# Token mixing of a hybrid decoder layer: the keys undivided until after the scores, and the turns of a tile moved behind them

## Chip, cores and metric

The kernel runs on one NeuronCore of a Trainium2 chip. The metric is the device time of one execution in microseconds (us); lower is better. The kernel before takes 2807.51 us, the median of three executions (2806.45 to 2814.20).

## The reference

One decoder layer over 2048 tokens of width 1024, in float32. One input projection feeds an RWKV-7 group (8 heads of 64) and a sliding-window attention group (8 query heads of 64, window 128). An output projection, a squared-ReLU MLP of width 4096 and a gated per-layer embedding follow. What the change touches is the RWKV group:

```python
kk = (k * k_k).reshape(B, S, H, N)
kk = kk / jnp.maximum(jnp.linalg.norm(kk, axis=-1, keepdims=True), 1e-12)
k = k * (1.0 + (a - 1.0) * k_a)
# per token and head, state is 64 x 64
sa = einsum('bhvk,bhk->bhv', state, -kk_t)
state = state * w_t + sa * (kk_t * a_t) + v_t * k_t
y = einsum('bhvk,bhk->bhv', state, r_t)
# after a group norm of y:
y = y + sum(r * k * r_k, axis=-1) * v
```

## The kernel before

**The work.** The kernel computes the scan in chunks of 64 tokens, two chunks in a tile of 128 tokens, 16 tiles in all. In a tile the decayed factors are called alpha (minus the key kk, times a decay), beta (kk times a, times the inverse decay), kappa (the modified key k, times the inverse decay) and rho (r, times a decay). Their pairwise products are the scores; masked, they give a triangular matrix per head and chunk that is inverted in blocks of 32 in five levels (products `mz0` to `mz4` on PE, L709; `z`, `up` and a transpose on DVE, L1499 to L1506), then joined to 64 (`q`, `b`, `xt64`). Then `uw`, `sa0`, `grow0`, `sa1`, `grow1` carry the state through the two chunks, and `y`, a group norm, `out` and `rw` end the tile. Attention of the same 128 tokens runs in between: `att0`, `att1` (L613), the soft maximum on DVE and ACT, and `pv` (L621).

**Large products.** The projection, the output product, the MLP and the gate (called the fill) are products of 128x128 by 128x512 in a split of each operand into a high and a low part, three products each (L590 to L594, L824 to L828, L866 to L870). A weight chunk of 512 KB is loaded three chunks ahead by SP (L376), its high part is written by ACT (L986) and its low part by DVE (L1300). The fill works in blocks of 512 tokens: `proj` 0 to 3, then `fin` 0 to 3.

**The order.** Every engine runs the same interleaving, written out by hand. `whole_program` runs `proj(0)` alone, then `proj(1)` to `proj(3)` beside the mixing of tiles 0 to 3, then `fin(b - 1)` beside the four tiles of block b, and `fin(3)` alone. A tile is a generator of 28 steps (`MIX_STEPS`), the fill is a generator of slots, most of them 12 large products on PE. The tuples `BESIDE_PROJ` (4 tiles) and `BESIDE_FIN` (4 tiles, used for three blocks) say for each step how many slots of the fill precede it. Steps of equal number have nothing of the fill between them. Each engine is in order, so a step whose input is late holds up all that stands behind it on that engine.

**The steps of a tile before the change.** Step 0: ACT tanh and sigmoid on the loaded rows (L1085, L1086), DVE the raw key (L1426), ACT its square (L1088). Step 1: PE `lora` (L639, L640) and `gate` (L643). Step 2: PE `norm` (L650), sums of squares per head, behind a wait for ACT's `sw`; ACT root (L1097); DVE running sum of the decay (`cum`, L1430) and `ascale` (L1434). Step 3: DVE reciprocal (L1440), ACT spreads it over 512 columns into `alpha_t` (L1100) and computes the exponentials; DVE `cumx`, `kmod`, `v_t`. Step 4: PE `spread`, four transposes of the widened reciprocal (L657); DVE multiplies the raw key by it (`kk`, L1451), then `kka`. Step 5: DVE alpha, beta, rk, kappa (L1457 to L1465). Step 6: PE `bonus` (L664) and twelve transposes of beta, alpha, kappa (L627); DVE `ends`, `rho`. Step 7: DVE `yb` and the copies `alpha_t`, `kappa_t` out of the banks. Step 8: PE scores (L684), DVE masks (L1485). Step 9: PE `av` (L696) and `att0`; DVE `init` (L1492), the first level, and the first attention logits. Steps 10 to 14: the levels. 15 `q`, 16 `b`, 17 `pv`, 18 `uw` (L744, L749), 19 `sa0` (L757), 20 `grow0` (L765), 21 `sa1`, 22 `grow1` and the inner part of y, 23 `y`, 26 `out` and `rw`.

```python
def side_by_side(fill, tiles, places):
    given = 0
    for i, place in enumerate(places):
        while given < place:
            next(fill)
            given += 1
        next(tiles[i // MIX_STEPS])
```

PE uses four banks for a tile, M0 to M3; before the change the scores could overwrite them only once `yb`, `beta_t`, `alpha_t` and `kappa_t` were out.

## Time and profile before

| | |
|---|---|
| executions | 2807.51 us median, 2806.45 to 2814.20, three |
| the profiled execution | 2812.94 us, span 2810.9 us |
| PE busy | 98% of the span, 25170 products |
| DVE, ACT busy | 62%, 40% |
| granted clock of PE, mean | 0.990 |

Busy time of PE is the union of its products' modelled durations. Products overlap, so the cost of one is read from the distance between starts. In the page a row reads: line, engine, operation, output and inputs, shapes, count, busy time, mean, idle time before it and what ended that.

### The profile page before, as it was taken

How to read it: one execution, taken by the hardware profiler on the slowest of the kernel's cores; microseconds unless marked ns; L12 is line 12 of the kernel's file. 1: busy time of each engine (PE TensorE's matmuls, PEld its weight loads, DVE VectorE, ACT ScalarE, POOL GpSimd, SP SyncE). 2: the span in 40 equal slices, each digit the busy share in tenths (PEclk: the TensorE clock that was granted, in tenths of full speed). 3: DMA queues.
4: the chain of work that ended last, by engine and by line, in shares of the span. 5: the costliest groups of instructions: out<-in, count | busy, mean ns of one | idle time of the engine just before them, and what ended most of it. 6: DMA issues, size and time to landing. Idle time of an engine off the chain costs nothing.

```text
span 2810.9 us, 57536 instructions
## 1 busy us (share of the span) xinstructions
PE 2748.7 (98%) x25170; PEld 2225.7 (79%) x25170; DVE 1742.8 (62%) x2941; ACT 1110.4 (40%) x1871; POOL 0.2 (0%) x4
## 2 busy tenths in 40 slices
PE   8999999999999999999999999999999999999998
PEld 6877787777878787878787878777888788888876
DVE  5477776757666566685766666857575655444335
ACT  4344443344433342553333424633433344332225
POOL 0000000000000000000000000000000000000000
PEclk9999999999999999999999999999999999999999
DMA  6554544453233233442333233523232234333332
GB/s 197 149 168 113 167 118 132 120 169 109 81 101 101 86 98 96 150 145 87 104 96 98 83 103 128 159 76 110 87 105 84 88 115 157 98 97 97 95 101 75
DMA packets 376197, 319.13 MB, mean 114 GB/s; under 512 B 48747, under 2 KB 328460, under 8 KB 375948
## 3 DMA queue, kind: packets, MB, share of 16 engines
q1 hardware_dynamic: 372272, 312.63, 36.5%
q8 instruction: 198, 3.24, 0.5%
q10 hardware_dynamic: 3676, 2.84, 0.4%
q14 instruction: 51, 0.42, 0.0%
HBM read 277.65 MB, written 38.14 MB: 112 GB/s over the span
## 4 chain that ended last, share of the span: by engine, by line
PE 73%; DVE 3%; ACT 2%; DMA 1%; issue 1%; SPq 0%; ACTq 0%
PE ps L824 13%; PE ps L828 12%; PE ps L827 12%; PE ps L866 9%; PE ps L869 8%; PE ps L870 8%; PE ps L709 1%; DMA wraw_f<-in_w_gate 1%; PE ps L684 1%; PE ps L621 1%; PE ps L765 1%; PE ps L837 1%; PE ps L757 1%; PE ps L627 1%; PE ps L613 1%
## 5 line engine op out<-in xcount | busy, mean ns | idle before, releaser
L1300 DVE TENSOR_TENSOR w_lo<-wraw_f,w_hi 128x1024 fp32r<-128x1024 f32 x408 | 498.0, 1221 | 357.3 <-ACT w_hi L986 356.4
L986 ACT ACTIVATE w_hi<-wraw_f 128x1024 fp32r<-128x1024 f32 x408 | 430.2, 1054 | 624.2 <-PE ps L824 505.9
L824 PE MATMUL ps<-w_hi,h_hi 128*128 128x512 f32 x1280 | 518.4, 405 | 10.8 <-DVE act_lo L1642 10.0
L828 PE MATMUL ps<-w_hi,h_lo 128*128 128x512 f32 x1280 | 501.8, 392 | 0.0
L827 PE MATMUL ps<-w_lo,h_hi 128*128 128x512 f32 x1280 | 501.6, 392 | 0.0
L866 PE MATMUL ps<-act_hi,w_hi 128*128 128x512 f32 x1024 | 408.4, 399 | 1.5 <-DVE w_lo L1300 1.4
L869 PE MATMUL ps<-act_lo,w_hi 128*128 128x512 f32 x1024 | 399.2, 390 | 0.0
L870 PE MATMUL ps<-act_hi,w_lo 128*128 128x512 f32 x1024 | 398.9, 390 | 0.0
L824 PEld LDWEIGHTS ps<-w_hi,h_hi 128*128 128x128 f32 x1280 | 241.7, 189 | 67.8 <-issue 16.9
L828 PEld LDWEIGHTS ps<-w_hi,h_lo 128*128 128x128 f32 x1280 | 241.7, 189 | 53.0
L827 PEld LDWEIGHTS ps<-w_lo,h_hi 128*128 128x128 f32 x1280 | 242.0, 189 | 46.0 <-issue 0.3
L1180 ACT ACTIVATE h_hi<-tmp 128x512 fp32r<-128x512 f32 x128 | 80.8, 631 | 462.3 <-DVE tmp L1633 462.3
L866 PEld LDWEIGHTS ps<-act_hi,w_hi 128*128 128x128 f32 x1024 | 192.1, 188 | 46.3 <-issue 4.1
L870 PEld LDWEIGHTS ps<-act_hi,w_lo 128*128 128x128 f32 x1024 | 192.2, 188 | 41.1
L869 PEld LDWEIGHTS ps<-act_lo,w_hi 128*128 128x128 f32 x1024 | 192.4, 188 | 37.3
L1636 DVE TENSOR_TENSOR h_lo<-tmp,h_hi 128x512 fp32r<-128x512 f32 x128 | 88.7, 693 | 156.8 <-ACT tmp L1181 156.8
L1633 DVE SCALAR_TENSOR_TENSOR tmp<-ps,stage_f 128x512 f32<-128x512 f32 x128 | 88.2, 689 | 137.7 <-PE ps L870 135.6
L590 PE MATMUL ps<-act_hi,w_hi 128*128 128x512 f32 x320 | 132.4, 414 | 0.0
L824 PE MATMUL ps<-w_hi,act_hi 128*128 128x512 f32 x320 | 127.3, 398 | 2.7 <-DVE w_lo L1300 2.4
L590 PE MATMUL ps<-h_hi,w_hi 128*128 128x512 f32 x320 | 128.4, 401 | 0.5 <-DVE h_lo L1311 0.5
L593 PE MATMUL ps<-act_lo,w_hi 128*128 128x512 f32 x320 | 127.8, 399 | 0.0
L594 PE MATMUL ps<-act_hi,w_lo 128*128 128x512 f32 x320 | 127.4, 398 | 0.0
(227 smaller groups left out, 3939.2 us busy)
## 6 DMA issues: line engine op xcount, KB each, us to landing
wraw_f<-in_w_ff_up SPq DMA_DIRECT2D x256, 256.0 KB, 3.3
wraw_f<-in_w_ff_down SPq DMA_DIRECT2D x128, 512.0 KB, 3.8
wraw_f<-in_w_in SPq DMA_DIRECT2D x80, 512.0 KB, 4.4
zT<-tmp SPq DMA_DIRECT2D x80, 256.0 KB, 2.1
wraw_f<-in_w_out SPq DMA_DIRECT2D x32, 512.0 KB, 4.1
wraw_f<-in_w_gate SPq DMA_DIRECT2D x32, 512.0 KB, 4.5
zs<-zT SPq DMA_DIRECT2D x16, 896.0 KB, 6.5
h_lo<-mixT SPq DMA_DIRECT2D x4, 2048.0 KB, 8.0
```

Source lines behind the costliest of these rows:

```text
L590: mm = T.matmul(dst, wh, hi[:, k, :], start=(k == 0), stop=False)
L593: T.matmul(dst, wh, lo[:, k, :], start=False, stop=False)
L594: mm = T.matmul(dst, wl, hi[:, k, :], start=False, stop=(k == DK - 1))
L824: mm = T.matmul(ps[:, j, :], ah, wh, start=(first and k == 0), stop=False)
L827: T.matmul(ps[:, j, :], ah, wl, start=False, stop=False)
L828: mm = T.matmul(ps[:, j, :], al, wh, start=False, stop=(final and k == 1))
L866: mm = T.matmul(ps[:, bank, :], wh, act_hi[:, k, :], start=(k == 0), stop=False)
L869: T.matmul(ps[:, bank, :], wh, act_lo[:, k, :], start=False, stop=False)
L870: mm = T.matmul(ps[:, bank, :], wl, act_hi[:, k, :], start=False, stop=(k == DK - 1))
L986: S.activation(w_hi[:, n % 2, :], raw[:, n % 4, :], ACT.Copy).then_inc(w_hi_done, 1)
L1300: V.tensor_tensor(w_lo[:, n % 2, :], raw[:, n % 4, :], w_hi[:, n % 2, :].bitcast(F32), ALU.subtract).then_inc(w_lo_done, 1)
L1636: V.tensor_tensor(h_lo[:, i, :], tmp[:, i % 2, :], h_hi[:, i, :].bitcast(F32), ALU.subtract).then_inc(fin_dve.mark(f"h_lo{g}_{i}"), 1)
```

## The change

1. The key is not divided by its norm before the scores. ACT's root (`nrm`) and the spreading (`kk_wide`), PE's `spread` and DVE's `kk` are gone. `norm` joins step 1 and goes to bank M2; its wait for `sw` is gone.
2. The inverse square of the norm is a factor per row: `init` becomes four products with it instead of four copies, a product `corner` over the right half of each head's first score block is new, and the copies `sa0` and `sa1` out of the banks become products with it.
3. The scores stand in step 5, directly on the factors, and the twelve transposes of beta, alpha, kappa behind them in step 6, in front of `av`. The copies `alpha_t`, `kappa_t` (DVE) and `beta_t` (ACT) are in step 6 too.
4. `bonus` and `att0` stand behind `mz0` in step 7, with `yb` in step 7 on DVE.
5. A tile has 25 steps. Both tuples of places are new; SP's load of the next tile's rows (`load_rw`) stands in step 8 in place of 9, still behind `yb`. All later steps are renumbered by minus 3.

The diff, without the renumbered rest, indentation reduced:

```diff
-MIX_PE = (["lora", "gate", "norm", "spread", "bonus", "beta", "alpha", "kappa"] + upto("score", 4) + ["av", "att0", "mz0", "mz1", "att1",
+MIX_PE = (["lora", "gate", "norm"] + upto("score", 4) + ["beta", "alpha", "kappa", "av", "mz0", "bonus", "att0", "mz1", "att1",
            "mz2", "mz3", "mz4", "q", "b", "pv", "uw",
            "sa0", "grow0", "sa1", "grow1", "y_in", "y", "out"])
-MIX_ACT = ["tanh", "sig_g", "kk_sq", "sw", "av", "nrm", "kk_wide", "p_inc", "p_inv", "p_exc", "gate", "beta_t", "avt",
+MIX_ACT = ["tanh", "sig_g", "kk_sq", "sw", "av", "p_inc", "p_inv", "p_exc", "gate", "beta_t", "avt",
            "exp0", "esink0", "exp1", "esink1", "att", "y_rms"]
...
-MIX_DVE = (["kk_raw", "cum", "ascale", "kk_max", "kk_inv", "cumx", "kmod", "v_t", "kk", "kka", "alpha", "beta", "rk", "kappa", "ends", "rho", "yb", "alpha_t", "kappa_t"]
-           + upto("mask", 4) + ["init", "up0", "m0"] + logits_of(0) + level_of(1) + ["v_turn"] + level_of(2) + probs_of(0) + level_of(3) + logits_of(1)
-           + level_of(4) + [f"z{LEVELS}", "inv_t", "inv", "xt64", "q"] + probs_of(1)
+MIX_DVE = (["kk_raw", "cum", "ascale", "kk_max", "kk_inv", "cumx", "kmod", "kka", "v_t", "alpha", "beta", "rk", "kappa", "ends", "rho"]
+           + upto("mask", 4) + ["init", "up0", "m0", "alpha_t", "kappa_t", "corner"] + level_of(1) + logits_of(0) + ["yb", "v_turn"] + level_of(2)
+           + level_of(3) + probs_of(0) + level_of(4) + logits_of(1) + [f"z{LEVELS}", "inv_t", "inv", "xt64", "q"] + probs_of(1)
            + ["b", "wT", "sa0", "grow0", "state0", "sa1", "grow1", "state1", "y_sum", "y_mean", "y", "y_sq", "y_var", "y_inv", "y_norm", "rw", "rw_yb", "rw_gate"])
-MIX_STEPS = 28
+MIX_STEPS = 25
...
-BESIDE_PROJ = (5, 6, 6, 6, 6, 6, 8, 9, 12, 15, 17, 19, 19, 21, 24, 26, 27, 29, 30, 31, 32, 33, 34, 34, 34, 35, 37, 37, 37, 39, 39,
-               39, 40, 40, 42, 42, 43, 44, 45, 46, 47, 49, 52, 55, 56, 58, 59, 61, 62, 63, 64, 64, 65, 65, 68, 69, 70, 73, 73, 75,
-               76, 76, 79, 79, 80, 81, 83, 84, 85, 86, 87, 88, 89, 90, 90, 90, 90, 91, 92, 92, 93, 93, 95, 97, 97, 98, 98, 98, 98,
-               98, 100, 101, 102, 103, 104, 106, 107, 109, 111, 112, 113, 114, 114, 114, 114, 115, 116, 116, 117, 118, 119, 119)
-BESIDE_FIN = (0, 1, 2, 4, 4, 4, 6, 6, 8, 9, 10, 12, 13, 15, 19, 23, 24, 26, 29, 31, 33, 35, 36, 37, 37, 38, 39, 39, 40, 40, 41, 46,
-               46, 46, 48, 48, 49, 50, 52, 53, 54, 55, 58, 61, 62, 64, 65, 67, 68, 69, 70, 70, 72, 72, 73, 74, 74, 75, 76, 80, 80,
-               80, 82, 82, 84, 85, 87, 91, 95, 97, 100, 102, 103, 104, 105, 106, 107, 108, 109, 109, 110, 110, 112, 113, 113, 114,
-               114, 117, 120, 125, 127, 133, 134, 135, 136, 137, 138, 140, 141, 142, 143, 144, 145, 146, 148, 149, 150, 150, 151,
-               153, 158, 158)
+BESIDE_PROJ = (4, 6, 6, 7, 7, 10, 12, 15, 16, 18, 20, 22, 24, 26, 27, 28, 29, 30, 32, 33, 33, 34, 35, 36, 37, 37, 40, 40, 41, 42, 44,
+               45, 45, 46, 47, 49, 50, 51, 53, 54, 55, 56, 57, 58, 59, 59, 59, 59, 61, 62, 63, 64, 64, 65, 65, 68, 70, 71, 74, 75,
+               76, 77, 79, 80, 81, 82, 83, 84, 85, 86, 86, 87, 87, 89, 90, 91, 92, 92, 93, 93, 96, 99, 100, 101, 103, 104, 105, 107,
+               109, 110, 111, 112, 113, 114, 115, 115, 117, 118, 119, 119)
+BESIDE_FIN = (0, 2, 2, 3, 4, 6, 7, 8, 9, 11, 13, 18, 21, 22, 24, 26, 27, 28, 31, 33, 33, 33, 35, 37, 39, 40, 40, 40, 42, 42, 44, 46,
+               47, 48, 49, 50, 52, 57, 58, 60, 61, 65, 66, 67, 70, 70, 73, 73, 76, 78, 78, 78, 78, 79, 79, 82, 83, 84, 86, 89, 93,
+               96, 99, 102, 105, 106, 109, 110, 111, 112, 112, 113, 114, 116, 116, 117, 122, 122, 123, 127, 130, 133, 134, 135, 136,
+               137, 138, 139, 140, 142, 144, 146, 147, 148, 149, 149, 151, 156, 158, 158)
...
             load_qkv(t + 1)
-        if step == 9 and t < TILES - 1:
+        if step == 8 and t < TILES - 1:
             sp.wait_ge(*mix_pe.done(t, "gate"))
             sp.wait_ge(*mix_dve.done(t, "yb"))
             load_rw(t + 1)
-        if step == 19:
...
     mm.then_inc(mix_pe.mark("gate"), 1)
-    yield
-    after(mix_act, "sw")
     after(mix_act, "kk_sq")
     for f in range(PAIRS):
-        mm = T.matmul(ps[:, M3, 2 * f:2 * f + 2], four(T1)[:, f, :], ones[:, 0:P:HD], start=True, stop=True)
+        mm = T.matmul(ps[:, M2, 2 * f:2 * f + 2], four(T1)[:, f, :], ones[:, 0:P:HD], start=True, stop=True)
     mm.then_inc(mix_pe.mark("norm"), 1)
     yield
     yield
-    after(mix_act, "kk_wide")
-    for f in range(PAIRS):
-        mm = T.transpose(ps[:, M3, f * P:(f + 1) * P], alpha_t[:, f * P:(f + 1) * P], ident)
-    mm.then_inc(mix_pe.mark("spread"), 1)
     yield
     yield
     after(mix_act, "gate")
-    after(mix_dve, "rk")
-    T.matmul(ps[:, M0, :], ones[:, :], work[:, KK, :], start=True, stop=True).then_inc(mix_pe.mark("bonus"), 1)
-    tokens_major("beta", M1, four(AV))
-    tokens_major("alpha", M2, pp[:, 0, :, :])
-    after(mix_dve, "kappa")
-    tokens_major("kappa", M3, four(KM))
-    yield
-    yield
-    after(mix_dve, "yb")
     after(mix_dve, "rho")
-    after(mix_dve, "v_t")
-    after(mix_act, "beta_t")
-    after(mix_dve, "alpha_t")
-    after(mix_dve, "kappa_t")
     for g in range(2):
         for f in (2 * g, 2 * g + 1):
             for src, at in ((four(AV), 0), (four(KM), 2 * CH)):
...
     after(mix_dve, "mask1")
     after(mix_dve, "mask2")
     after(mix_dve, "mask3")
+    tokens_major("beta", M1, four(AV))
+    tokens_major("alpha", M2, pp[:, 0, :, :])
+    tokens_major("kappa", M3, four(KM))
...
     mm.then_inc(mix_pe.mark("av"), 1)
-    pe.wait_ge(qkv_in, 16 * (2 + P // SUB) * (t + 1))
-    scores(0)
     yield
     for l in range(LEVELS):
...
         mm.then_inc(mix_pe.mark(f"mz{l}"), 1)
+        if l == 0:
+            after(mix_dve, "kappa_t")
+            T.matmul(ps[:, M3, :], ones[:, :], work[:, KK, :], start=True, stop=True).then_inc(mix_pe.mark("bonus"), 1)
+            after(mix_act, "beta_t")
+            pe.wait_ge(qkv_in, 16 * (2 + P // SUB) * (t + 1))
+            scores(0)
         if l == 1:
             after(mix_dve, "logit0")
             scores(1)
...
-        if step == 2:
-            after(mix_pe, "norm")
-            S.activation(knorm[:, :], ps[:, M3, 0:HEADS], ACT.Sqrt).then_inc(mix_act.mark("nrm"), 1)
         if step == 3:
-            after(mix_dve, "kk_inv")
-            S.activation(alpha_t[:, :].rearrange("p (h d) -> p h d", h=HEADS), over(knorm[:, :], HD), ACT.Copy).then_inc(
-                mix_act.mark("kk_wide"), 1)
             after(mix_dve, "cum")
...
             if t:
                 act.wait_ge(att_stored, 16 * t)
             S.activation(pp[:, 0, :, :], four(SW), ACT.Exp, scale=-DECAY).then_inc(mix_act.mark("p_exc"), 1)
-        if step == 4:
             if t:
                 act.wait_ge(*mix_dve.done(t - 1, "rw_gate"))
             copy("gate", gate[:, :, :], ps[:, M1, :].rearrange("p (f t) -> p f t", f=PAIRS), "gate")
         if step == 6:
             copy("beta_t", beta_t[:, :], ps[:, M1, :], "beta")
-        if step == 9:
+        if step == 6:
             copy("avt", avt, ps[:, M0, :], "av")
-        if step in (10, 13):
-            exps(step // 13)
-        if step == 17:
+        if step in (8, 11):
+            exps(step // 11)
+        if step == 14:
...
     def chunk_of_sa(c):
         after(mix_pe, f"sa{c}")
-        V.tensor_copy(sa[tok64(c), :].rearrange("p (f a v) -> p a f v", a=2, v=HD),
-                      ps[tok64(c), M2:M2 + 2, 0:PAIRS * HD].rearrange("p a (f v) -> p a f v", f=PAIRS)).then_inc(mix_dve.mark(f"sa{c}"), 1)
+        key = knorm[tok64(c), :].rearrange("p (f a) -> p a f", a=2).unsqueeze(3).broadcast_to([CH, 2, PAIRS, HD])
+        V.tensor_tensor(sa[tok64(c), :].rearrange("p (f a v) -> p a f v", a=2, v=HD),
+                        ps[tok64(c), M2:M2 + 2, 0:PAIRS * HD].rearrange("p a (f v) -> p a f v", f=PAIRS), key,
+                        ALU.mult).then_inc(mix_dve.mark(f"sa{c}"), 1)
     def chunk_of_state(c):
         after(mix_pe, f"grow{c}")
...
-        if step == 3:
-            after(mix_act, "nrm")
-            V.tensor_scalar(knorm[:, :], knorm[:, :], 1e-12, None, ALU.max).then_inc(mix_dve.mark("kk_max"), 1)
+            after(mix_pe, "norm")
+            V.tensor_scalar(knorm[:, :], ps[:, M2, 0:HEADS], 1e-24, None, ALU.max).then_inc(mix_dve.mark("kk_max"), 1)
             own("kk_max")
             V.reciprocal(knorm[:, :], knorm[:, :]).then_inc(mix_dve.mark("kk_inv"), 1)
+        if step == 3:
...
+            own("kk_raw")
+            V.tensor_tensor(four(AV), four(KK), four(AV), ALU.mult).then_inc(mix_dve.mark("kka"), 1)
...
             V.transpose(v_t[:, :], kappa_t[:, :]).then_inc(mix_dve.mark("v_t"), 1)
         if step == 4:
-            after(mix_pe, "spread")
-            V.tensor_tensor(work[:, KK, :], work[:, KK, :], ps[:, M3, :], ALU.mult).then_inc(mix_dve.mark("kk"), 1)
-            own("kk")
-            V.tensor_tensor(four(AV), four(KK), four(AV), ALU.mult).then_inc(mix_dve.mark("kka"), 1)
-        if step == 5:
             after(mix_act, "p_exc")
-            own("kk")
             V.scalar_tensor_tensor(pp[:, 0, :, :], four(KK), -1.0, pp[:, 0, :, :], ALU.mult, ALU.mult).then_inc(mix_dve.mark("alpha"), 1)
             after(mix_dve, "kka")
             V.tensor_tensor(four(AV), four(AV), four(PINV), ALU.mult).then_inc(mix_dve.mark("beta"), 1)
...
             o.then_inc(mix_dve.mark("rk"), 1)
             own("rk")
             V.tensor_tensor(four(KM), four(KM), four(PINV), ALU.mult).then_inc(mix_dve.mark("kappa"), 1)
-        if step == 6:
             V.tensor_copy(ends[:, :, :], pp[:, 1, :, :].rearrange("p f (c t) -> p f c t", c=2)[:, :, :, CH - 1]).then_inc(
                 mix_dve.mark("ends"), 1)
             own("ends")
             V.tensor_tensor(pp[:, 1, :, :], r, pp[:, 1, :, :], ALU.mult).then_inc(mix_dve.mark("rho"), 1)
-        if step == 7:
-            after(mix_pe, "bonus")
-            if t:
-                dve.wait_ge(*mix_dve.done(t - 1, "rw_gate"))
-            V.tensor_tensor(yb[:, :, :], ps[:, M0, :].rearrange("p (f t) -> p f t", f=PAIRS), v, ALU.mult).then_inc(mix_dve.mark("yb"), 1)
-            after(mix_pe, "alpha")
-            V.tensor_copy(alpha_t[:, :], ps[:, M2, :]).then_inc(mix_dve.mark("alpha_t"), 1)
-            after(mix_pe, "kappa")
-            own("v_t")
-            V.tensor_copy(kappa_t[:, :], ps[:, M3, :]).then_inc(mix_dve.mark("kappa_t"), 1)
-        if step == 8:
+        if step == 5:
...
-        if step == 9:
+        if step == 6:
             own("mask3")
+            own("kk_inv")
             for i in range(4):
                 at = (i % 2) * SUB
-                o = V.tensor_copy(xx[sub32(i), 1, :, :].rearrange("p (a f) t -> p f a t", a=2),
-                                  bm[sub32(i), :, 0, at:at + SUB].rearrange("p (f a) t -> p f a t", a=2))
+                o = V.tensor_tensor(xx[sub32(i), 1, :, :].rearrange("p (a f) t -> p f a t", a=2),
+                                    bm[sub32(i), :, 0, at:at + SUB].rearrange("p (f a) t -> p f a t", a=2),
+                                    over(knorm[sub32(i), :], SUB).rearrange("p (f a) t -> p f a t", a=2), ALU.mult)
             o.then_inc(mix_dve.mark("init"), 1)
-        if 9 <= step < 9 + LEVELS:
-            l = step - 9
+        if 6 <= step < 6 + LEVELS:
+            l = step - 6
...
-        if step == 9:
+        if step == 6:
+            after(mix_pe, "alpha")
+            V.tensor_copy(alpha_t[:, :], ps[:, M2, :]).then_inc(mix_dve.mark("alpha_t"), 1)
+            after(mix_pe, "kappa")
+            own("v_t")
+            V.tensor_copy(kappa_t[:, :], ps[:, M3, :]).then_inc(mix_dve.mark("kappa_t"), 1)
+            own("init")
+            V.tensor_tensor(bm[:, :, 0, SUB:], bm[:, :, 0, SUB:], over(knorm[:, :], SUB), ALU.mult).then_inc(mix_dve.mark("corner"), 1)
+        if step == 7:
             logits(0)
-        if step == 10:
+            after(mix_pe, "bonus")
+            if t:
+                dve.wait_ge(*mix_dve.done(t - 1, "rw_gate"))
+            V.tensor_tensor(yb[:, :, :], ps[:, M3, :].rearrange("p (f t) -> p f t", f=PAIRS), v, ALU.mult).then_inc(mix_dve.mark("yb"), 1)
...
```

## Rows read from the trace of the kernel before

**Rows 1.** The page, busy time of each engine.

```profile
PE 2748.7 (98%) x25170; PEld 2225.7 (79%) x25170; DVE 1742.8 (62%) x2941; ACT 1110.4 (40%) x1871; POOL 0.2 (0%) x4
```

**Rows 2.** Waits of PE: who waited for whom, us in total, times, longest.

```profile
PE ps L639 <- ACT zs L1086: 7.1, 2, 4.0
PE ps L657 <- ACT alpha_t L1100: 4.3, 2, 2.6
...
PE ps L765 <- DVE work L1407: 1.6, 2, 0.8
PE ps L757 <- DVE work L1551: 1.6, 2, 0.8
PE ps L744 <- ACT pp L1080: 1.6, 2, 0.8
PE ps L560 <- DVE rw L1582: 1.5, 1, 1.5
```

**Rows 3.** Windows: busy time of PE, PEld, DVE, ACT, POOL; granted clock, DMA.

```profile
153.00:167.00 14.00, 11.87 (x50) 10.36 (x51) 10.53 (x26) 11.93 (x24) 0.00 (x0) 0.51 0.57 184
458.00:500.00 42.00, 39.22 (x301) 32.03 (x300) 30.06 (x63) 20.34 (x32) 0.00 (x0) 0.89 0.32 89
556.00:564.00 8.00, 6.43 (x73) 5.19 (x67) 3.45 (x5) 1.06 (x1) 0.00 (x0) 0.79 0.39 106
600.00:618.00 18.00, 14.92 (x68) 12.21 (x68) 10.06 (x15) 13.62 (x22) 0.00 (x0) 0.81 0.71 254
618.00:1120.00 502.00, 497.70 (x5322) 399.95 (x5322) 324.15 (x558) 184.30 (x323) 0.00 (x0) 1.00 0.32 95
```

**Rows 4.** Timeline of PE in the first tile: start, us, what, idle before.

```profile
149.05 0.39 PE L594 MATMUL ps<-act_hi,w_lo 128*128 128x512 f32 x1
153.43 0.58 PE L639 MATMUL ps<-zs,lora 64*128 64x128 f32 x1 [3.99 <-ACT zs L1086]
```

**Rows 5.** Timeline of SP at the same place.

```profile
138.78 0.39 SPq L403 DMA_DIRECT2D zs<-zT  x1
```

**Rows 6.** DMA issues from 130 to 160 us, KB, us to landing.

```profile
zs<-zT SPq DMA_DIRECT2D x1, 896.0 KB, 5.8
```

**Rows 7.** Timeline of ACT at the same place.

```profile
149.08 1.06 ACT L986 ACTIVATE w_hi<-wraw_f 128x1024 fp32r<-128x1024 f32 x1 [4.44 <-DMA wraw_f<-in_w_in]
```

**Rows 8.** Timeline of PE, large products right after the stall at 489 us.

```profile
493.43 0.63 PE L593 MATMUL ps<-act_lo,w_hi 128*128 128x512 f32 x1
493.86 0.63 PE L594 MATMUL ps<-act_hi,w_lo 128*128 128x512 f32 x1
```

**Rows 9.** Timeline of PE around one spread.

```profile
624.60 0.39 PE L827 MATMUL ps<-w_lo,h_hi 128*128 128x512 f32 x1
624.83 0.39 PE L828 MATMUL ps<-w_hi,h_lo 128*128 128x512 f32 x1
...
625.72 0.39 PE L827 MATMUL ps<-w_lo,h_hi 128*128 128x512 f32 x1
```

**Rows 10.** Timeline of PE around one mz product.

```profile
1222.22 0.39 PE L828 MATMUL ps<-w_hi,h_lo 128*128 128x512 f32 x1
1222.54 0.75 PE L709 MATMUL ps<-work,small 32*32 32x32 f32 x64
1223.23 0.50 PE L824 MATMUL ps<-w_hi,h_hi 128*128 128x512 f32 x1
1223.56 0.39 PE L827 MATMUL ps<-w_lo,h_hi 128*128 128x512 f32 x1
```

**Rows 11.** Timeline of PE, gate of the fourth tile.

```profile
487.16 1.16 PE L643 MATMUL ps<-zs,gup 128*128 128x128 f32 x8
```

**Rows 12.** Timeline of DVE there, from cum to kappa (11 groups between them lie close).

```profile
488.45 1.37 DVE L1430 TENSOR_TENSOR_SCAN work<-con,work 128x128 f32<-128x128 f32 x4
...
497.43 0.69 DVE L1465 TENSOR_TENSOR work<-work 128x512 f32<-128x512 f32 x1
498.04 1.22 DVE L1300 TENSOR_TENSOR w_lo<-wraw_f,w_hi 128x1024 fp32r<-128x1024 f32 x1
```

More of the change, by code:

```diff
@@ L448, in mix @@
                     for step in range(MIX_STEPS):
-                        if step == 14 and t < TILES - 1:
+                        if step == 11 and t < TILES - 1:
                             sp.wait_ge(*mix_pe.done(t, "att1"))
                             load_qkv(t + 1)
-                        if step == 9 and t < TILES - 1:
+                        if step == 8 and t < TILES - 1:
                             sp.wait_ge(*mix_pe.done(t, "gate"))
@@ L455, in mix @@
                             load_rw(t + 1)
-                        if step == 19:
+                        if step == 16:
                             sp.wait_ge(*mix_act.done(t, "att"))
                             sp.dma_start(mixT[PAIRS:, :, t * P:(t + 1) * P].rearrange("f p t -> p f t"), attT).then_inc(att_stored, 16)
-                        if step == 23 and t < TILES - 1:
+                        if step == 20 and t < TILES - 1:
                             sp.wait_ge(*mix_pe.done(t, "grow1"))
                             load_v(t + 1)
-                        if step == 27:
+                        if step == 24:
                             sp.wait_ge(*mix_dve.done(t, "rw_gate"))
@@ L1514, in mix @@
                                 mix_dve.mark("v_turn"), 1)
-                        if step == 11:
+                        if step == 9:
                             probabilities(0)
-                        if step == 12:
+                        if step == 10:
                             own("pt0")
                             logits(1)
-                        if step == 9 + LEVELS:
+                        if step == 6 + LEVELS:
                             after(mix_pe, f"mz{LEVELS - 1}")
@@ L1533, in mix @@
                                             ALU.mult).then_inc(mix_dve.mark("xt64"), 1)
-                        if step == 15:
+                        if step == 12:
                             after(mix_pe, "q")
@@ L1539, in mix @@
                             o.then_inc(mix_dve.mark("q"), 1)
-                        if step == 15:
+                        if step == 12:
                             probabilities(1)
-                        if step == 16:
+                        if step == 13:
                             after(mix_pe, "b")
@@ L1548, in mix @@
                             o.then_inc(mix_dve.mark("b"), 1)
-                        if step == 18:
+                        if step == 15:
                             after(mix_pe, "uw")
@@ L1552, in mix @@
                                           ps[:, M0:M0 + 2, 0:256].rearrange("p c (f t) -> p c f t", f=PAIRS)).then_inc(mix_dve.mark("wT"), 1)
[L1553 removed]
+                        if step == 16:
                             chunk_of_sa(0)
+                        if step == 17:
+                            chunk_of_state(0)
+                        if step == 18:
+                            chunk_of_sa(1)
                         if step == 20:
[L1556 to L1559 removed]
                             chunk_of_state(1)
@@ L1577, in mix @@
                             V.tensor_tensor(y3, y3, over(yvar[:, :], HD), ALU.mult).then_inc(mix_dve.mark("y_norm"), 1)
-                        if step == 26:
+                        if step == 23:
                             after(mix_pe, "out")
```

11 lines of the change are left out of this document (3 added, 8 removed).

## Prediction

> **What bounds the kernel now.** The page first: PE is busy for 98% of the span, DVE for 62%, ACT for 40% [rows 1]. So the time is PE's own work and the places at which PE stands. The waits of PE come next: in the tiles they are few and large [rows 2], 4.0 and 3.1 us (7.1 together) for the sigmoid at the head of a tile (L639), 2.6 and 1.7 for the widened norm (L657), and three kinds of 0.8, twice each, in the run uw, sa0, grow0. The windows show what follows such a stall: the granted clock falls [rows 3]. From 153 to 167 us it is 0.51, so PE runs at the lower of its two levels (1.2 and 2.4 GHz) nearly throughout; from 458 to 500 us the mean is 0.89, from 556 to 564 us 0.79, from 600 to 618 us 0.81. At the lower level large products start 0.43 us apart [rows 8], at the upper 0.23 [rows 10]; a stretch of w us at mean clock c costs w times (1 - c). All of this lies in the projection stage and at the start of the first finishing block. From 618 to 1120 us PE is busy 497.7 of 502 us at full clock [rows 3]; there is next to nothing to win in the later blocks but PE's own work.
>
> **The sum, part by part.** Working against the profiled execution, 2812.9 us (span 2810.9, 2 us around it); it lies 5.4 us above the median of 2807.5, and I carry the difference over unchanged.
>
> *Products on PE.* I price an insertion into the fill as the distance from the last large product ahead of it to the second behind it, less two spacings of 0.227 us. The spread: 625.72 - 624.83 - 0.45 = 0.44 us [rows 10]; 16 tiles, minus 7.0. Bonus, the twelve turns, scores, av, both att and all levels stay and only change neighbours. Norm joins lora and gate: full-array products beside full-array products start at the usual distance, so this is nothing, except that its wait for `sw` goes. But bonus, a full-array product, now stands between mz0 and att0, which use parts of the array. At such a border the row shows 0.32 us (1222.22 to 1222.54) and on the other side 0.33 (1223.23 to 1223.56) where 0.23 is usual [rows 11]: 0.1 each. Before, the groups on parts of the array were scores, av with att0, and mz0, three; now they are scores, av, mz0, and att0, four, so there is one pair of borders more. Plus 0.2 x 16 = 3.3 us; bounds 0 and twice that. Together minus 3.7.
> The Trainium skill (TensorEngine Tiling (Array Packing), Key Properties) says that changing the tiling mode drains TensorE. Taken as the full 0.39 us of a product on both sides of the new pair it would make this part plus 5.5 instead of minus 3.7; the row shows 0.1 a side.
>
> *The head of the first tile.* PE reaches lora at 149.3 us and stands until 153.43 [rows 4]. ACT runs step 0 from 150.1, because the weight split ahead of it (149.08) had waited 4.44 us for its load [rows 7]; step 0 takes 3.3 us (150.14 to 153.43). The rows that step 0 needs were issued at 138.8 to 139.2 [rows 5] and land 5.8 us later [rows 6], at 145.0. Step 0 moves from place 5 to 4, ahead of that split. It then runs in ACT's idle time, 145 to 148.3, and PE does not stand: minus 4.0. The spread's wait (1.7) goes with the spread, and so does the low clock, 14 x 0.49 = 6.8 us [rows 3]: minus 12.5. What is late next: the scores need rho, four slots behind norm, and DVE has the work of steps 2 to 4 plus weight splits and a late load; then the split for the next chunk stands behind rho. I set 2.5 us of new waits and 1.7 of clock (a stretch like that of 556 to 564 us, 8 x 0.21). Net minus 8.3; bounds minus 12.5 and minus 3.
>
> *The fourth tile.* Steps 1, 2, 4 were all at place 98. The wait of 2.6 for the widened norm goes, with the clock lost behind it: 42 x 0.11 = 4.6 us less 1.2 that belongs to the run before it, 3.4. Minus 6.0. The scores are now four slots behind, at 96.
>
> *The runs uw, sa0, grow0.* In two tiles these stood at one place (90 and 114) and PE waited three times 0.8; behind it 1.7 us of clock [rows 2, 3]. In the new tuples each has a slot of its own (82 to 85, 109 to 114). Two times 4.1: minus 8.2.
>
> *The head of the fifth tile.* Lora moves from place 1 to 2, one slot or 12 x 0.227 = 2.7 us, against a wait of 3.1, with 18 x 0.19 = 3.4 us of clock behind it. A wait of 0.4 is left: minus 6.0.
>
> *Small ones.* The wait at L560 (1.5) has a slot more; norm's wait for `sw` in the tiles where the two steps touched, and one level that stood at the place of another (19 and 19), go as well; I estimate 0.9 for each of these two, by the 0.8 of a wait between touching steps [rows 2]. Minus 3.3.
>
> *ACT and DVE.* ACT loses a root, a copy of 512 columns and a table load, DVE gains a product on 256 columns and four dearer copies and loses one of 512 columns. Neither engine is near full; I cost both at nothing, and the cover is the slots between the steps.
>
> *New waits.* The chain that must fit: gate starts at 487.16 [rows 9], cum at 488.45, kappa ends at 498.12 [rows 11, 12]. Without kk (0.7) and its waits (0.4), with ends and rho (0.85) and one weight split (1.2) [rows 12], rho is done at 499.1, with the shift of a projection slot (1.6 more of DVE work) at 500.7. PE has gate and norm (1.8) and four slots (10.9) and stands at the scores at 499.9. So 0 to 0.8 a tile, and only where fill work of DVE lies between steps 3 and 4; one such tile (place 42), plus 0.8. One tile has turns with av and mz0 at one place (45): mz0 waits for ACT's copy of av, bonus for kappa_t, plus 1.0. In each finishing block the first tile has steps 5 to 9 at 6, 7, 8, 9, 11 beside the four output additions: 1.0 a block, plus 3.0. Together plus 4.8; bounds 0 and 15.
>
> Sum: -3.7 - 8.3 - 6.0 - 8.2 - 6.0 - 3.3 + 4.8 = -30.7. Profiled 2782.2, median 2776.8, say **2777**. With the bounds of the unknown terms 2768 to 2791.
>
> **Rivals.**
> *A. The stalls move.* Old stalls came from several steps at one place and from chains that did not fit; the new tuples have the same kind of spots (scores always four slots behind norm, masks one slot behind scores). For it: the chain of rows 12 fits by less than a microsecond. Against it: rows 3 show that tuples of this kind can run 502 us with 4.3 us idle. If four such stalls of 2.5 us with 3 us of clock each come back, plus 22 less the 4.8 counted: 2794.
> *B. Small waits hold the clock down.* Three waits of 0.8 were enough for a stretch at the lower level [rows 2, 3]. The Trainium skill (TensorE: Matmul & The Clock Gate, A second HAM failure mode) describes just this, PE idling briefly between groups so often that the clock swings. Here: each projection tile gets such a cluster between scores and mz0, 4 x (2.4 + 1.7) less what I counted: 2790. The trace agrees that short waits can do it.
> *C. Slower: the scores wait for rho.* The scores used to have the copies, now they have only the chain of step 4 ahead of them. If rho were late by 1.6 us at every tile's scores, and each such wait cost 1.7 of clock as well: 16 x 3.3 = 53, less the 31 won and the 4.8 counted: about 2824. It decides from a lateness of some 1.3 us in every tile. Against it: the page shows DVE at 62%, and in the finishing blocks DVE has less to do in the slots.
> *D. Every border drains.* By the rule named above and as a mechanism of PE here, 0.8 us a tile in place of 0.2, and the same at the new border of turns and av: plus 16: 2793. Rows 11 speak against it.
> *E. The change wins only its products.* The stalls are of the first 620 us and of loads, and places do not matter: 2804.
>
> **Chances.** Forecast 0.60, A 0.17, B 0.07, C 0.06, D 0.04, E 0.06. About 0.3%, 8.4 us, is what a measurement of this kernel can tell from no change, so faster means under 2799.1: forecast, B, D and most of A, 0.85; within 0.3%: E and the rest of A, 0.09; slower 0.06. The range goes from the best sum, and 2 us for the spread of executions, to A and a little over: 2765 to 2798.
>
> **What would show it.** Right: no L657; L639 with no wait of microseconds at 150 and 607 us; granted clock 1.00 from 153 to 167, 458 to 500 and 556 to 564 us; no waits of PE at L744, L757, L765; two groups of scores and turns in the new order, and the first PE product of finishing blocks some 20 us earlier; finishing blocks shorter by 1 to 2 us each. Wrong: waits of PE for DVE's rho or masks at the scores and the turns, or a granted clock under 1 in new stretches; the distance at bonus well above 0.43 on its far side.

## The result and the profile after

The changed kernel takes 2767.07 us (median of four executions, 2766.94 to 2768.69) against 2806.98 us (four, 2804.68 to 2814.20): a ratio of 0.9855, 95% interval 0.9837 to 0.9873, or 40 us. The profiled executions are 2768.69 and 2812.94 us, 44.3 us apart; the sum of the prediction was made against the latter and gave 30.7.

The page after, span and busy times [rows 1]:

```profile
span 2766.9 us, 57315 instructions
PE 2725.0 (98%) x25106; PEld 2208.2 (80%) x25106; DVE 1736.6 (63%) x2941; ACT 1080.9 (39%) x1823; POOL 0.2 (0%) x4
```

PE's busy time fell by 23.7 us, the rest of the span by 20.3. The waits of PE after (who waited for whom, us in total, times, longest) [rows 2]:

```profile
PE ps L567 <- DVE stage_f L1283: 10.9, 3, 8.3
PE ps L589 <- DVE w_lo L1277: 4.2, 3, 3.1
PE ps L713 <- DVE small L1515: 2.5, 3, 0.8
PE ps L808 <- DVE act_lo L1619: 2.5, 1, 2.5
PE ps L808 <- DVE w_lo L1277: 2.3, 3, 0.8
PE ps L808 <- ACT tmp L1212: 1.6, 2, 1.3
PE ps L692 <- DVE kappa_t L1478: 1.0, 3, 0.3
PE ps L687 <- DVE small L1472: 0.9, 4, 0.4
PE ps L687 <- ACT work L1064: 0.7, 1, 0.7
...
PE ps L638 <- ACT zs L1070: 0.4, 1, 0.4
PE ps L661 <- DVE pp L1444: 0.2, 1, 0.2
```

L567 is the start of the program. Lora (L638) waits 0.4 where it waited 7.1; the uw, sa0, grow0 lines and the row of L560 (the transposes of the next block's input) are not in the list any more; the scores (L661) wait 0.2 for rho in all 16 tiles together. New are L589, a low weight part late by 3.1 us in the first tile, L713, the product `b` behind the copy of `q` in the first tile of each finishing block (0.8 each), and L692, bonus behind kappa_t. The levels (L687) wait 1.6 us, where they waited 1.9 (L709). L808 behind ACT's tmp is 1.6 where it was 0.2, but in e5 below it is 0.2 again.

The windows after at the places of [rows 3] and at two more (busy times of PE, PEld, DVE, ACT, POOL; granted clock, DMA share, GB/s):

```profile
15.00:23.00 8.00, 7.21 (x25) 5.62 (x24) 7.50 (x12) 5.68 (x9) 0.00 (x0) 0.57 0.84 303
147.00:165.00 18.00, 14.87 (x79) 11.92 (x78) 10.17 (x23) 12.00 (x23) 0.00 (x0) 0.93 0.81 267
440.00:500.00 60.00, 59.94 (x637) 48.72 (x630) 47.34 (x100) 26.88 (x48) 0.00 (x0) 1.00 0.45 129
545.00:565.00 20.00, 19.94 (x203) 16.65 (x202) 12.33 (x22) 6.15 (x8) 0.00 (x0) 1.00 0.50 138
600.00:1100.00 500.00, 498.28 (x5435) 401.57 (x5435) 324.89 (x560) 177.21 (x311) 0.00 (x0) 1.00 0.34 97
2650.00:2655.00 5.00, 4.41 (x12) 3.52 (x13) 2.26 (x3) 1.14 (x2) 0.00 (x0) 0.66 0.49 164
```

Where tiles are mixed, the clock is full but for the first tile. From 147 to 165 us the loss is 18 x 0.07 = 1.3 us, and with the rest of that stretch, up to 166 us (0.57 from 162 to 166), 1.7 us, where it was 6.8. The two other stretches are not of the change: one is in the start of the program (15 to 23 us, 0.57; the profiled execution of the kernel before has 1.00 there, so the changed kernel comes to the first tile 0.65 us later), the other is in the last block, in both kernels (0.66 from 2650 to 2655 us, and before 0.57 from 2696 to 2700).

What the prediction had not seen is in the finishing blocks. Timeline of PE where the embedding input is transposed (L913 before, L897 after), first the kernel before, with its row of the waits of PE:

```profile
PE ps L824 <- DVE act_lo L1642: 10.0, 4, 2.5
```

```profile
1055.81 1.03 PE L913 MATMUL ps<-con,line 128*128 128x128 f32 x8
1059.35 0.47 PE L824 MATMUL ps<-w_hi,h_hi 128*128 128x512 f32 x1 [2.51 <-DVE act_lo L1642]
```

and after:

```profile
1026.85 1.03 PE L897 MATMUL ps<-con,line 128*128 128x128 f32 x8
1027.72 0.60 PE L626 MATMUL ps<-con,work 128*128 128x128 f32 x4
...
1029.13 1.15 PE L676 MATMUL ps<-v_t,bm 64*64 64x64 f32 x32
1030.41 0.47 PE L808 MATMUL ps<-w_hi,h_hi 128*128 128x512 f32 x1
```

PE used to stand 2.51 us for the low part of that input in each of the four blocks (10.0 us together, the longest row of its waits but for the start of the program). Now the turns and av of the last tile stand right behind the transposes and fill the time; only in the last block, which has no tile beside it, is the wait left (2.5, L808). The same point of the program is reached at 1026.85 in place of 1055.81 us, so 29.0 of the 44.0 us of span were won ahead of the first of these waits and 15.0 behind it. By the first large product of each finishing block (604.82, 1185.21, 1761.38 and 2337.63 us before, 585.17, 1154.37, 1723.53 and 2293.70 after) the blocks are shorter by 11.2, 7.0, 6.1 and 0.0 us. In the second block of the kernel before the clock was lost as well:

```profile
1634.21 0.52 PE L824 MATMUL ps<-w_hi,h_hi 128*128 128x512 f32 x1 [2.51 <-DVE act_lo L1642]
1634.52 0.63 PE L827 MATMUL ps<-w_lo,h_hi 128*128 128x512 f32 x1
1634.95 0.63 PE L828 MATMUL ps<-w_hi,h_lo 128*128 128x512 f32 x1
```

The large products stand 0.43 us apart there until 1637.92, as they do from 2211.34 to 2213.89 in the third block, some 3 us each. In the first block the same wait was not followed by this (1.00 from 1059 to 1066 us).

### The profile page after: what moved, and what is told of

It is laid out like the page before. It is cut to its first block, busy times and chain, and to the rows that moved or that the text cites. A ratio compares the mean times of both kernels' runs of the same rounds, so it can differ in the third digit from the quotient of the medians.

```text
span 2766.9 us, 57315 instructions
## 1 busy us (share of the span) xinstructions
PE 2725.0 (98%) x25106; PEld 2208.2 (80%) x25106; DVE 1736.6 (63%) x2941; ACT 1080.9 (39%) x1823; POOL 0.2 (0%) x4
## 4 chain that ended last, share of the span: by engine, by line
PE 82%; DVE 2%; ACT 2%; DMA 1%; issue 1%; SPq 0%; ACTq 0%
PE ps L808 13%; PE ps L811 12%; PE ps L812 12%; PE ps L850 9%; PE ps L853 8%; PE ps L854 8%; PE ps L589 3%; PE ps L592 2%; PE ps L593 2%; PE ps L687 2%; DMA wraw_f<-in_w_gate 1%; PE ps L661 1%; PE ps L620 1%; PE ps L612 1%; PE ps L749 1%; PE ps L741 1%
## 5 line engine op out<-in xcount | busy, mean ns | idle before, releaser
L808 PE MATMUL ps<-w_hi,h_hi 128*128 128x512 f32 x1280 | 513.2, 401 | 2.9 <-DVE act_lo L1619 2.5
L853 PE MATMUL ps<-act_lo,w_hi 128*128 128x512 f32 x1024 | 399.1, 390 | 0.0
L854 PE MATMUL ps<-act_hi,w_lo 128*128 128x512 f32 x1024 | 399.0, 390 | 0.0
L808 PEld LDWEIGHTS ps<-w_hi,h_hi 128*128 128x128 f32 x1280 | 240.5, 188 | 61.3 <-issue 10.7
L589 PE MATMUL ps<-act_hi,w_hi 128*128 128x512 f32 x320 | 129.5, 405 | 4.2 <-DVE w_lo L1277 4.2
L808 PE MATMUL ps<-w_hi,act_hi 128*128 128x512 f32 x320 | 127.1, 397 | 4.1 <-DVE w_lo L1277 2.3
L589 PE MATMUL ps<-h_hi,w_hi 128*128 128x512 f32 x320 | 129.4, 404 | 0.5 <-DVE h_lo L1288 0.5
L592 PE MATMUL ps<-h_lo,w_hi 128*128 128x512 f32 x320 | 125.6, 392 | 0.0
L593 PE MATMUL ps<-h_hi,w_lo 128*128 128x512 f32 x320 | 125.5, 392 | 0.0
```

What stands on the lines that cost most here:

```text
L589: mm = T.matmul(dst, wh, hi[:, k, :], start=(k == 0), stop=False)
L592: T.matmul(dst, wh, lo[:, k, :], start=False, stop=False)
L593: mm = T.matmul(dst, wl, hi[:, k, :], start=False, stop=(k == DK - 1))
L808: mm = T.matmul(ps[:, j, :], ah, wh, start=(first and k == 0), stop=False)
L853: T.matmul(ps[:, bank, :], wh, act_lo[:, k, :], start=False, stop=False)
L854: mm = T.matmul(ps[:, bank, :], wl, act_hi[:, k, :], start=False, stop=(k == DK - 1))
```

## The experiments

The runs were made in three sets, each beside the kernel before on the same chip: 2810.23 us for e1, e2, e3 and e5, 2809.01 for e6 and e7, 2809.29 for e4, e8, e9 and e11. A distance to the changed kernel, which was timed in a set of its own, is given twice: by the ratios to the kernel before, and by the medians.

### e11: the spread's products put back

```diff
                     mm.then_inc(mix_pe.mark("norm"), 1)
                     yield
                     yield
+                    after(mix_act, "sw")
+                    for f in range(PAIRS):
+                        mm = T.transpose(ps[:, M3, f * P:(f + 1) * P], zs[:, 8 + f, :], ident)
+                    mm.then_inc(mix_pe.mark("ballast"), 1)
```

> The changed kernel with four transposes of 128 columns put back in step 2 of every tile, of rows that are there, into a bank that nobody reads: the spread's products without its wait for a widened norm. Theory 1 (0.44 us a tile): 7 us slower than the changed kernel, about 2774. Rival (off the path in the gaps of PE): within 2 us.

2774.00 us, ratio 0.9874 (0.9858 to 0.9889): 5.3 us above the changed kernel by the ratios, 6.9 by the medians; the two intervals overlap a little. The sizes fit PE's own work being the path and 16 x 0.44 us being the price of the spread without its wait.

### e5: bonus behind att0

```diff
-                            after(mix_dve, "kappa_t")
-                            T.matmul(ps[:, M3, :], ones[:, :], work[:, KK, :], start=True, stop=True).then_inc(mix_pe.mark("bonus"), 1)
+                            after(mix_dve, "alpha_t")
                             after(mix_act, "beta_t")
                             pe.wait_ge(qkv_in, 16 * (2 + P // SUB) * (t + 1))
                             scores(0)
+                            after(mix_dve, "kappa_t")
+                            T.matmul(ps[:, M3, :], ones[:, :], work[:, KK, :], start=True, stop=True).then_inc(mix_pe.mark("bonus"), 1)
...
-                            logits(0)
                             after(mix_pe, "bonus")
+                            logits(0)
```

> The changed kernel with bonus behind att0 in step 7 and not between mz0 and att0; DVE waits for bonus before the first logits. PE then goes from one product on parts of the array to the next and has one pair of borders less. Theory 1 (a border costs 0.1 us a side, nothing more): 0.2 us a tile, and 1.0 us less waiting for kappa_t, 3 to 5 us faster than the changed kernel, about 2763. Rival (a border drains the array, 0.8 us a tile): 11 to 14 us faster. Second rival (the logits start 0.9 us later, att1 waits for them): no faster or up to 5 us slower.

2763.34 us, ratio 0.9838 (0.9821 to 0.9854), 4.8 us under the changed kernel by the ratios, 3.7 by the medians; the two intervals overlap. Timeline of PE in the changed kernel at mz0, bonus, att0:

```profile
489.12 0.39 PE L593 MATMUL ps<-act_hi,w_lo 128*128 128x512 f32 x1
...
490.12 1.12 PE L692 MATMUL ps<-work,ones 128*128 128x512 f32 x2
491.18 0.61 PE L612 MATMUL ps<-kT,qT 64*32 64x160 f32 x20
```

Bonus to att0 is 1.06 us. Bonus is two instructions: their starts are 0.54 us apart, and att0 starts 0.52 behind the second, where in the kernel before, between products on the full array, both distances are 0.43. So the border costs 0.1 us on each side. From the last large product ahead of the group to the second behind it are 3.10 us in the changed kernel (489.12 to 492.22) and 2.89 in e5 (486.93 to 489.82). The wait for kappa_t is gone from the waits of e5. This is the 0.2 us a tile of the forecast and not the 0.8 of a full drain. Of the rule in the Trainium skill (TensorEngine Tiling (Array Packing), Key Properties), the direction is seen, as 0.1 us a border; rival D falls.

### e1: turns ahead of the transposes of the embedding input

```diff
-               96, 99, 102, 105, 106, 109, 110, 111, 112, 112, 113, 114, 116, 116, 117, 122, 122, 123, 127, 130, 133, 134, 135, 136,
+               96, 99, 102, 105, 106, 109, 110, 111, 112, 112, 113, 114, 116, 116, 117, 122, 122, 123, 127, 130, 132, 134, 135, 136,
```

> The changed kernel with one number of its places altered: in the finishing blocks the last tile's step 6 (turns and av) stands at 132 in place of 133, so ahead of the transposes of the embedding input and not behind them. Theory 1 (the change won some 11 us in the finishing blocks because turns and av now cover PE's wait for the low part of that input): the wait of 2.5 us comes back in three blocks and with it a stretch at the lower clock level in some, so 7.5 to 13 us slower than the changed kernel, about 2777. Rival (the gain there comes from the shorter chain of the tile as a whole): within 2 us of the changed kernel, 2767 to 2769.

2783.33 us, ratio 0.9906 (0.9891 to 0.9921): 14.3 us slower than the changed kernel by the ratios, 16.3 by the medians. The wait of PE for act_lo in e1, and its timeline at the first of the places:

```profile
PE ps L808 <- DVE act_lo L1619: 14.6, 4, 4.0
```

```profile
1029.85 1.09 PE L897 MATMUL ps<-con,line 128*128 128x128 f32 x8
1034.98 0.77 PE L808 MATMUL ps<-w_hi,h_hi 128*128 128x512 f32 x1 [4.03 <-DVE act_lo L1619]
1035.54 0.63 PE L811 MATMUL ps<-w_lo,h_hi 128*128 128x512 f32 x1
1035.97 0.63 PE L812 MATMUL ps<-w_hi,h_lo 128*128 128x512 f32 x1
```

14.6 less 2.5 us are 12.1 us more of waiting, 4.0 in each of three blocks and not 2.5, and behind 1034.98 the products stand 0.43 us apart, the lower clock. So at these places this one number is worth 14 to 16 us, more than the 7.5 to 13 that I expected. It is more than the cover: the step that moved has DVE work in it too (init, the first level, two copies and `corner`, 1030.09 to 1034.15 us), and DVE now runs that ahead of the low part for which PE waits (L1619, at 1034.15), where it ran the low part first.

### e2: can the kernel before have the same cover?

```diff
-               114, 117, 120, 125, 127, 133, 134, 135, 136, 137, 138, 140, 141, 142, 143, 144, 145, 146, 148, 149, 150, 150, 151,
+               114, 117, 120, 125, 127, 133, 133, 135, 136, 137, 138, 140, 141, 142, 143, 144, 145, 146, 148, 149, 150, 150, 151,
```

> The kernel before with one number altered: in the finishing blocks the last tile's step 8 (scores) stands at 133 in place of 134, right behind the transposes of the embedding input. Theory 1: the scores' 2.1 us of products cover 2.1 of the 2.55 us of idle time in three blocks, minus 6.4 us, and the lower clock at 1634 and 2211 us (3.4 us each, half of it lost) goes too: 6 to 10 us faster than before, about 2798. Rival (the wait only moves, as the scores then wait for the copies out of the banks or the masks come late): within 2 us of before.

2817.97 us, ratio 1.0033 (1.0020 to 1.0046): slower, by 8 us. Waits of PE, and PE and DVE at the first place:

```profile
PE ps L684 <- DVE kappa_t L1480: 14.7, 3, 4.9
```

```profile
1054.81 1.28 DVE L1642 TENSOR_TENSOR act_lo<-ps,act_hi 128x512 fp32r<-128x512 f32 x2
1056.01 0.68 DVE L1475 TENSOR_TENSOR yb<-ps,zs 128x512 f32<-128x512 f32 x1
1056.61 0.68 DVE L1477 COPY alpha_t<-ps 128x512 f32<-128x512 f32 x1
...
1057.20 0.68 DVE L1480 COPY kappa_t<-ps 128x512 f32<-128x512 f32 x1
1058.03 3.27 PE L684 MATMUL ps<-pp,work 64*64 64x128 f32 x64 [4.90 <-DVE kappa_t L1480]
```

The scores of the kernel before wait for yb, alpha_t and kappa_t, which DVE runs behind the very low part (L1642) whose wait was to be covered. They cover nothing and wait 4.9 us, three times. The mechanism of the rival was right, though it gave 2 us at most: a cover must not hang on the engine that is late.

### e3 and e4: the kernel before at mended places

```diff
-BESIDE_PROJ = (5, 6, 6, 6, 6, 6, 8, 9, 12, 15, 17, 19, 19, 21, ...
+BESIDE_PROJ = (4, 6, 6, 6, 7, 7, 9, 9, 12, 15, 17, 18, 19, 21, ...
...
-               76, 76, 79, 79, 80, 81, 83, 84, 85, 86, 87, 88, 89, 90, 90, 90, 90, 91, 92, 92, 93, 93, 95, 97, 97, 98, 98, 98, 98,
+               74, 74, 77, 77, 78, 79, 80, 81, 82, 83, 84, 85, 86, 87, 88, 89, 90, 91, 92, 92, 93, 93, 95, 96, 96, 97, 97, 98, 99,
...
-BESIDE_FIN = (0, 1, 2, 4, 4, 4, 6, 6, 8,
+BESIDE_FIN = (0, 2, 2, 4, 4, 4, 6, 6, 8,
```

This is e4; in the fourth tile the steps behind score stand one slot apart as well. e3 has the spread and bonus of the first and third tile elsewhere, and e2's edit.

> The kernel before, its 28 steps and all its products unchanged, with new places only: no two dependent steps of PE at one place in uw, sa0, grow0; spread a slot or more behind norm in tiles 0 to 3; step 0 of the first tile at 4; lora of each finishing block at 2; scores right behind the transposes of the embedding input. Theory 1 (the change won by the stalls that it removed, and a mere 4 us by its products): 28 to 38 us faster than before, 2770 to 2780. Rival 2 (the shorter chain of the tile is what makes room, places alone cannot remove the stalls): they move on, less than 15 us faster, over 2792.

> The kernel before, steps and products unchanged, second try at places: the scores stay at 134; no two of uw, sa0, grow0 at one place; spread a slot behind norm in tiles 0 and 3; the third tile two slots earlier; lora of each finishing block at 2. Theory 1 (places alone remove the stalls of the first 620 us): 15 to 25 us faster than before, about 2788. Theory 2 (28 steps with spread and with scores behind the copies leave no room, the waits turn up at spread, bonus, scores or at the weight splits): within 8 us of before, with waits of PE at L650, L657 or L677 together over 5 us.

e3: 2822.06 us, ratio 1.0044 (1.0029 to 1.0058), 12 us slower than before; in it the scores wait 16.3 us for kappa_t, as in e2. e4: 2805.14 us, ratio 0.9986 (0.9976 to 0.9996), 4 us faster than before. Waits of PE in e4:

```profile
PE ps L817 <- DVE act_lo L1635: 10.0, 4, 2.5
PE ps L650 <- ACT alpha_t L1093: 5.8, 2, 5.3
PE ps L643 <- ACT work L1086: 3.4, 10, 1.4
...
PE ps L657 <- DVE work L1455: 2.0, 2, 1.3
```

The runs uw, sa0, grow0 are gone from the list, but spread (L650) waits 5.8, norm (L643) 3.4 for `sw`, bonus (L657) 2.0. With 28 steps and these chains the waits changed places. Two tuples by hand do not show that none is better; they show that taking the slots apart as I did is not enough.

### e6: step 0 of the first tile alone

```diff
-BESIDE_PROJ = (5, 6, 6,
+BESIDE_PROJ = (4, 6, 6,
```

> The kernel before with one number altered: step 0 of the first tile at place 4 in place of 5, ahead of the weight split that waits 4.4 us for its load. Theory 1: tanh and sigmoid run while ACT is idle, PE does not stand at lora at 149 us, minus 4.0 us and up to 3.4 of clock; the wait for the widened norm stays: 4 to 7 us faster than before. Rival (the load of the next weights is late anyway, so PE stands a few us later in place of there): within 2 us of before, with a wait of PE for the low part of a weight chunk of 3 us or more near 155 to 162 us.

2810.92 us, ratio 1.0003 (0.9993 to 1.0013): nothing. Waits of PE and DVE between 140 and 165 us:

```profile
PE ps L657 <- ACT alpha_t L1100: 7.7, 1, 7.7
...
DVE tmp L1349 <- DMA zT<-tmp: 4.2, 1, 4.2
```

Lora no longer waits there, as forecast, but the spread now waits 7.7 us in its stead, behind a DVE that stands 4.2 us until the store of the last z chunk has left its buffer. The rival (it only moves) was right in the time, but the wait is behind a store, and not, as it said, for the low part of a weight chunk.

### e7: turns ahead of the scores again

```diff
                     after(mix_dve, "rho")
+                    tokens_major("beta", M1, four(AV))
+                    tokens_major("alpha", M2, pp[:, 0, :, :])
+                    tokens_major("kappa", M3, four(KM))
+                    after(mix_act, "beta_t")
+                    after(mix_dve, "alpha_t")
+                    after(mix_dve, "kappa_t")
...
                     after(mix_dve, "mask3")
-                    tokens_major("beta", M1, four(AV))
-                    tokens_major("alpha", M2, pp[:, 0, :, :])
-                    tokens_major("kappa", M3, four(KM))
```

> The changed kernel with part 3 undone: the twelve turns of beta, alpha, kappa stand in step 5 ahead of the scores, which wait for the three copies out of the banks; places as in the changed kernel. Theory 1: PE's products are the same, but the scores wait for alpha_t and kappa_t, two copies of 0.69 us behind the last turns, and DVE may still be at rho when alpha is ready: 1.0 to 1.8 us of waiting a tile, 16 to 29 us, and half a stretch of 3.4 us of lower clock in the tiles where the wait is long enough (up to 27 us): 2785 to 2820. Rival (the copies are hidden behind the turns themselves, and the scores are late because of rho in any case): within 6 us of the changed kernel.

2817.59 us, ratio 1.0030 (1.0020 to 1.0039): 49 us slower than the changed kernel by the ratios, 51 by the medians. Waits of PE:

```profile
PE ps L667 <- DVE kappa_t L1453: 36.5, 16, 6.3
PE ps L811 <- DVE act_lo L1622: 6.8, 4, 2.5
```

In each of the 16 tiles the scores wait for kappa_t, 36.5 us together; the cover of the embedding input is gone too. At these 25 steps and places the gain needs the order scores, then turns.

### e8: the changed steps at the old places

```diff
-BESIDE_FIN = (0, 2, 2, 3, 4, 6, 7, 8, 9, 11, 13, 18, 21, 22, 24, 26, 27, 28, 31, 33, 33, 33, 35, 37, 39,
+BESIDE_FIN = (0, 1, 2, 4, 4, 8, 9, 10, 12, 13, 15, 19, 23, 24, 26, 29, 31, 33, 35, 36, 37, 37, 38, 39, 39,
```

and so on in both tuples: the old entries of steps 4, 6 and 7 are left out.

> The changed kernel with the places of the kernel before, the entries of steps 4, 6 and 7 left out of both tuples (so scores, turns with av, and mz0 with bonus and att0 stand where scores, av with att0, and mz0 stood). It shows what the changed steps win without new places. Both theories: products 4 us, no wait for the widened norm (4.3 us and 3 to 5 of clock); the stalls in uw, sa0, grow0, at the head of the fifth tile and behind the transposes of the embedding input stay. 10 to 18 us faster than before, 2790 to 2798; so 22 to 30 us of the change would need the new places. If instead it is over 35 us faster, the places did nothing.

2826.77 us, ratio 1.0057 (1.0039 to 1.0075): 17 us slower than before, and I had expected 10 to 18 faster. Waits of PE:

```profile
PE ps L802 <- DVE act_lo L1613: 10.0, 4, 2.5
PE ps L815 <- DVE x L1581: 7.8, 3, 2.7
PE ps L632 <- ACT zs L1064: 7.4, 2, 4.4
PE ps L844 <- DVE w_lo L1271: 6.6, 9, 1.1
PE ps L583 <- DVE w_lo L1271: 6.5, 4, 3.8
PE ps L802 <- DVE w_lo L1271: 5.1, 7, 0.8
```

All the old stalls but the spread's are there, and those of the fill have grown: 18.2 us for low weight parts (L844, L583, L802), where it was 4.5 before, and 7.8 for an output addition that DVE runs behind the logits, where it was 1.4. Steps now hold more DVE work (alpha to rho in one, masks and copies near each other), and at the old places this stands ahead of what the fill needs; I read that from one such place, at 669 us, and did not follow the others.

### e9: the x tiles loaded one by one

On top of e5:

```diff
-                        if f == 0 and b < BLOCKS - 1:
-                            load_x_tiles(b + 1)
+                        if f < TPB and b < BLOCKS - 1:
+                            load_x_tiles(b + 1, f)
```

> The changed kernel with bonus behind att0 and SP loading the four x tiles of the next block one in each of the first four projection chunks in place of all four in the first. Theory 1 (PE's wait of 3 us for a low weight part at 158 us comes from 2 MB of x in the queue ahead of the weights and of the stored z): the wait shrinks to under 1 us and the stretch of lower clock at 162 us goes, 3 to 5 us faster than with bonus behind att0 alone (2763), about 2759. Rival (the load is late for another reason, as the rows, keys and values of the first tile are ahead of it too): within 1.5 us of 2763.

2758.81 us, ratio 0.9816 (0.9800 to 0.9831), the fastest of all: 11.0 us under the changed kernel by the ratios, 8.3 by the medians, and 6.2 or 4.5 under e5, where the intervals still overlap. First the changed kernel around 158 us, the DVE and the PE that wait:

```profile
156.51 0.69 DVE L1326 TENSOR_TENSOR tmp<-line 128x512 f32<-128x512 f32 x1 [4.27 <-DMA zT<-tmp]
```

```profile
161.80 0.50 PE L589 MATMUL ps<-act_hi,w_hi 128*128 128x512 f32 x1 [3.13 <-DVE w_lo L1277]
```

and the window of e9:

```profile
147.00:165.00 18.00, 18.00 (x147) 14.97 (x150) 14.16 (x33) 15.68 (x29) 0.00 (x0) 1.00 0.77 251
```

PE is busy 18.0 of 18 us at full clock, where it was 0.93. The wait for a low weight part did not shrink to under 1 us, as I had expected: 1.6 us of it are left, at 167.03, behind the window. In the changed kernel the 2 MB of x were issued ahead of the store that DVE waits for and of the weights. With the x tiles apart both come in time: DVE waits 0.3 us for the store and not 4.3, ACT 0.5 for the weights and not 4.5.

## Why the prediction was right, and where its steps failed

The time was in the range and the direction as forecast, but I gave 31 us for a gain of 40 (44 in the profiled executions), and 2767.07 lies only 2 us inside the fast end of the range. That it lies inside is in part luck: the term that was missing stood in none of the bounds. The bounds of the sum, 2768 to 2791, do not come out of its terms either: all at their best give 2764.5, all at their worst 2795.6. The prediction also names some groups of rows one too high or too low: the spread's rows are 9, the borders' 10 and the gate's 11. By its steps:

- **Products, -3.7.** Held. e11 measured the spread at 5.3 to 6.9 us for 7.0, and the timelines of e5 and the changed kernel show the 0.2 us of the extra pair of borders.
- **Head of the first tile, -8.3.** The old wait went and new ones came, as written. Rows: 3.1 us at L589 and 1.7 us of clock, with 1.0 of smaller waits at the next steps, against 2.5 and 1.7. But the reason given, step 0 one slot earlier, is not enough: by e6 that alone wins nothing, as the spread then waits 7.7 us, and in e4, with a slot between norm and spread, it still waits 5.3. The changed order has no PE step that needs a chain of DVE and ACT before four slots have passed; that this is what makes it work is my reading of the three traces.
- **Fourth tile, the runs uw, sa0, grow0, fifth tile, -20.2.** These waits are gone and the clock is 1.00 in the windows. That new places would remove them holds for the changed kernel, not by themselves: e4 won 4 us and e3 lost 12.
- **New waits, +4.8.** L713, L692 and L661 wait 2.5 + 1.0 + 0.2 = 3.7 us; the levels waited as long before. The 3.0 us for the first tiles of the finishing blocks came as 2.5, though at the product `b` and not in steps 5 to 9. The chain to rho fitted its four slots: L661 waits 0.2 in all, which ends rival C.
- **"There is next to nothing to win in the later blocks."** This is the step that failed, the term of the sum that was missing. I read 4.3 us of idle time in 502 and passed over the wait for act_lo, 2.5 us in each of the four finishing blocks, and expected these blocks to be shorter by 1 to 2 us each, where the first three are by 11.2 (some 6 of it lora's wait and the clock behind it), 7.0 and 6.1. 15.0 us of the gain came behind the first arrival at that place: three of these waits, 7.5; clock behind two of them, some 3.4 (twice 3.4 us at half speed); the products of the eight tiles left, 8 x 0.23 = 1.8; and 2.3 that I did not take apart (it is not in the other waits behind that point, which are 6.6 us before and 7.2 after). e1 puts this one place at 14 to 16 us, with the DVE work that moves along; the cover by itself is the 7.5 and the 3.4.

Rivals A and B did not come: at the new places neither the stalls nor the low clock were back, but for the 3.1 us at L589 and its 1.7 of clock. Rival E (the places do not matter) is refuted from both sides: the changed steps at the old places are 17 us slower than before (e8), the old steps at mended places 4 us faster (e4). The gain of 40 is neither a sum of the two nor of single waits. Fewer steps, scores with no copies ahead of them (e7), and places made for them came near it only together. What stays open: how much the row factor alone gives with the old order and places made for that, and how much the old 28 steps give at places better than the two tried here (e3, e4); no run settles either.

## What to carry to other kernels

When the busiest engine is 98% busy, list its few waits with what each costs in clock behind it, in every stage, and look for a group of its own work that needs nothing from the late engine to put right there. A step moved without the chain that feeds it moves its wait; before counting a wait as won, name the next one that the same late engine, buffer or store will cause. Treat a change of steps and the places of the steps as one edit: here the steps alone lost 17 us, the places alone won 4 at best, and both together won 40.
